# A PEER layer with 112 instead of 96 tokens gathered, and a dense pass over 144 instead of 160

## The reference, cut to what matters

```python
def peer(h, w_pq, sub_keys, u_tab, v_tab):
    qr = (hb @ w_pq).reshape(b, t, PEER_HEADS, 2, PEER_DKEY // 2)
    sc = jnp.einsum('bthpd,hpnd->bthpn', qr, sub_keys)
    s_top, i_top = lax.top_k(sc, PEER_TOPK)                 # 16 of 128, twice
    cand = s_top[..., 0, :, None] + s_top[..., 1, None, :]
    c_top, c_pos = lax.top_k(cand.reshape(b, t, PEER_HEADS, 256), PEER_TOPK)
    ...
    expert = i0 * PEER_NKEYS + i1                           # 8 heads x 16 picks = 128 per token
    g = jax.nn.softmax(c_top, axis=-1)
    a = jax.nn.gelu(jnp.einsum('bthkd,btd->bthk', u_tab[expert], hb))
    return jnp.einsum('bthk,bthkd->btd', (g * a), v_tab[expert])
```

## Time and profile before

| | |
|---|---|
| median of 3 runs | 1709.11 us (1707.29 to 1711.14) |
| profiled execution, its own time | 1709.63 us |
| its span in the trace | 1707.7 us |
| PE busy | 1668.3 us (98%) |
| VectorE busy | 1017.4 us (60%) |
| ScalarE, GpSimd busy | 405.2 us (24%), 262.2 us (15%) |
| moved by DMA | 569.87 MB, 334 GB/s over the span |
| granted TensorE clock | 0.994 |

### The profile page before, as it was taken

How to read it: one execution, slowest core, us unless ns; L and a number is a source line. 1 busy time by engine, 2 the same in 40 slices (tenths; PEclk the granted TensorE clock), 3 DMA queues, 4 the chain that set the end, 5 groups by cost and what they waited for, 6 DMA issues and landing times.

```text
span 1707.7 us, 28225 instructions
## 1 busy us (share of the span) xinstructions
PE 1668.3 (98%) x11296; PEld 1587.6 (93%) x11296; DVE 1017.4 (60%) x1695; ACT 405.2 (24%) x1027; POOL 262.2 (15%) x252
## 2 busy tenths in 40 slices
PE   7999999999999999999999999999989999999999
PEld 6768888888999999999899999999989999999998
DVE  5325695766778999767677676373335443443331
ACT  6547567646441000021112111210000000000000
POOL 1020000000003322231312221031112111111100
PEclk9999999999999999999999999999999999999999
DMA  9665446476548999999999999799999999999995
GB/s 354 215 145 145 127 137 196 137 232 211 173 159 354 422 394 422 405 406 417 393 407 424 397 423 423 296 362 421 422 413 422 422 422 422 422 421 422 422 368 174
DMA packets 106476, 569.87 MB, mean 334 GB/s; under 512 B 11184, under 2 KB 13360, under 8 KB 47472
## 3 DMA queue, kind: packets, MB, share of 16 engines
q1 hardware_dynamic: 56480, 216.51, 34.6%
q0 software_dynamic: 31792, 220.50, 31.9%
q10 hardware_dynamic: 18144, 132.13, 18.9%
HBM read 563.04 MB, written 4.46 MB: 332 GB/s over the span
## 4 chain that ended last, share of the span: by engine, by line
PE 64%; DMA 18%; DVE 13%; issue 2%; POOL 1%; ACT 1%; SPq 0%; DVEq 0%; ACTq 0%; POOLq 0%
PE ps L1516 32%; DMA late<-in_u_rows,sel 8%; PE ps L1461 6%; PE ps L1263 5%; PE ps L1265 5%; PE ps L1264 5%; DMA sel<-sel 5%; DVE late L1097 3%; DMA acts<-in_u_rows,sel 3%; PE ps L1282 2%; PE ps L1419 2%; PE ps L1418 2%; PE ps L1417 2%; DVE w_lo L788 1%; DMA raw<-in_w_in 1%
## 5 line engine op out<-in xcount | busy, mean ns | idle before, releaser
L1101 DVE SCALAR_TENSOR_TENSOR acts<-late,sel,acts 128x2048 f32<-128x2048 f32 x77 | 181.0, 2351 | 240.1 <-DMA late<-in_v_tab,sel 239.6
L1516 PE MATMUL ps<-acts,raw 128*128 (+1 forms) x2048 | 285.8, 301 | 5.9 <-DMA raw<-in_v_tab 5.9
L1461 PE MATMUL ps<-acts,late 128*128 128x160 f32 x2048 | 290.5, 301 | 0.0
L1516 PEld LDWEIGHTS ps<-acts,raw 128*128 128x128 f32 x2048 | 282.2, 191 | 6.1 <-issue 6.1
L1461 PE MATMUL ps<-acts,raw 128*128 128x160 f32 x2048 | 286.7, 299 | 0.0
L1461 PEld LDWEIGHTS ps<-acts,late 128*128 128x128 f32 x2048 | 284.4, 192 | 0.0
L1516 PE MATMUL ps<-acts,late 128*128 (+1 forms) x2048 | 284.2, 299 | 0.0
L1461 PEld LDWEIGHTS ps<-acts,raw 128*128 128x128 f32 x2048 | 280.4, 190 | 0.2 <-DMA raw<-in_u_tab 0.2
L1516 PEld LDWEIGHTS ps<-acts,late 128*128 128x128 f32 x2048 | 280.1, 190 | 0.1
L788 DVE TENSOR_TENSOR w_lo<-raw,w_hi 128x512 fp32r<-128x512 f32 (+1 forms) x288 | 189.0, 683 | 140.8 <-ACT w_hi L530 139.4
L1097 DVE SCALAR_TENSOR_TENSOR late<-late,acts 128x2048 f32<-128x2048 f32 x76 | 173.3, 2289 | 54.3 <-DMA late<-in_u_rows,sel 54.1
(11 more groups left out here) (207 smaller groups left out, 1522.0 us busy)
## 6 DMA issues: line engine op xcount, KB each, us to landing
raw<-in_w_in SPq DMA_DIRECT2D x72, 512.0 KB, 3.7
raw<-in_u_tab SPq DMA_DIRECT2D x33, 1024.0 KB
late<-in_u_tab SPq DMA_DIRECT2D x33, 1024.0 KB
raw<-in_v_tab SPq DMA_DIRECT2D x32, 1024.0 KB
raw<-in_v_tab ACTq DMA_DIRECT2D x32, 1024.0 KB
late<-in_v_tab SPq DMA_DIRECT2D x32, 1024.0 KB
late<-in_v_tab ACTq DMA_DIRECT2D x32, 1024.0 KB
raw<-in_u_tab ACTq DMA_DIRECT2D x31, 1024.0 KB
```

What stands on the lines that cost most here:

```text
L1101: V.scalar_tensor_tensor(acc, row[n % NROW], w_sp[:, n - N_OWN:n - N_OWN + 1], acc, ALU.mult, ALU.add).then_inc(row_used, 1)
L1461: ins = mm(ps[:, q, 0:N_DN], ring[q][:, k * P:k * P + P], hF[:, k, :], start=k == 0, stop=k == KD - 1)
L1516: ins = mm(ps[:, pair_bank(k // 2), at:at + N_DN], ring[q][:, k * P:k * P + P], acts[:, ds(i * (4 * N_DN) + q * N_DN, N_DN)], start=first ...
```

## The change

`SHARE` becomes 8: of eight partitions of tile 0 seven are gathered tokens and one is a helper. That makes 112 gathered and 144 dense tokens, `N_OWN` 112, `N_TURN` 16, seven turns, `N_GRP` 36 and `FIRST_G` 56. So there are 112 gathers of each table and 144 moving columns in each dense matmul. Beside that:

- the gate tables exist twice (`hot1[g % 2]`, `hot0[g % 2]`), and DVE writes those of group g+1 where it wrote those of g;
- 24 rows instead of 6 are taken ahead of the normalisation of the gates;
- a gather of the second table waits, beside its free buffer, until the chunks have come to a given number (from chunk 116 on, 134 chunks for 112 rows);
- the weights of the gathered tokens are made ready at chunk `WEIGH_AT` = 120 instead of 122, and from there one row is taken in each second chunk instead of each one;
- the score tiles lie elsewhere, so that one fill of ones on POOL goes; the turns are written as a loop.

```diff
-    SHARE = 4
+    SHARE = 8
@@
-        hot1 = early[:, 0:512].rearrange("p (t n) -> p t n", t=4)
-        hot0 = early[:, 512:1024].rearrange("p (t n) -> p t n", t=4)
+        hot1 = [at.rearrange("p (t n) -> p t n", t=4) for at in (early[:, 0:512], region(A_TK, 512))]
+        hot0 = [at.rearrange("p (t n) -> p t n", t=4) for at in (early[:, 512:1024], region(A_TK + 512, 512))]
@@
+        WEIGH_AT = NKEY - 8
+        PACE_FROM, PACE_TO = NKEY - 12, 2 * NKEY - 6
@@ def gather(n):
                 if n >= NROW:
                     pool.wait_ge(row_used, n + 1 - NROW)
+                if n >= N_OWN:
+                    pool.wait_ge(unit_used, PACE_FROM + (n - N_OWN) * (PACE_TO - PACE_FROM) // N_OWN)
@@ POOL
-            pool.memset(region(A_SCORE + 2048, 2048), 1.0).then_inc(ones_set, 1)
...
+            def next_turn(first, turn):
+
+                gathers(first, (turn - 1) * N_TURN + NROW - 1)
+                pool.wait_ge(row_used, (turn - 1) * N_TURN)
+                pool.dma_start(hs[turn % 2][helpers, :], hs[turn % 2][lenders[turn], :]).then_inc(hs_in, 16)
...
-            for i in range(2):
+            for i in range(SHARE - 2):
                 pool.wait_ge(turn_kept, i + 1)
                 pool.dma_start(lent[lenders[i], :], acc_copy[helpers, :]).then_inc(lent_in, 16)
@@ DVE
-            next_row(6)
+            next_row(24)
@@ def hots(g):
-                if g:
-                    dve.wait_ge(gate_mm, g)
-                for f, dst in ((1, hot1), (0, hot0)):
+                if g >= 2:
+                    dve.wait_ge(gate_mm, g - 1)
+                for f, dst in ((1, hot1[g % 2]), (0, hot0[g % 2])):
@@
             for c in range(FIRST_G + 4, NKEY):
                 if c % 2 == 0:
-                    hots(g)
+                    if g + 1 < N_GRP:
+                        hots(g + 1)
...
-                if c == NKEY - 6:
+                if c == WEIGH_AT:
...
-                if c > NKEY - 6:
+                if c > WEIGH_AT and c % 2:
                     next_row()
...
-            for turn in range(3):
+            for turn in range(SHARE - 1):
                 next_row(N_OWN + (turn + 1) * N_TURN - rows_done[0])
-                if turn < 2:
+                if turn < SHARE - 2:
```

More of the change, by code:

```diff
@@ L183, in build_block @@
         own_row, help_count = sel[:, 2 * N_PICK + N_OWN:2 * N_PICK + N_OWN + 1], sel[:, 2 * N_PICK + N_OWN + 1:2 * N_PICK + N_OWN + 2]
-        A_SCORE = NKEY * N_DN - TT * 2048
+        A_SCORE = [NKEY * N_DN - 2048, A_ROW + D + 1504]
+        assert A_SUBK + 16 * NKEY <= A_SCORE[0] and A_SCORE[1] + 2048 <= NKEY * SEQ
         A_TK = A_ROW + D
@@ L188, in build_block @@
         A_ONES = FIRST_G * N_DN
-        score = [region(A_SCORE + 2048 * b, 2048).rearrange("p (c n) -> p c n", c=16) for b in range(TT)]
+        score = [region(A_SCORE[b], 2048).rearrange("p (c n) -> p c n", c=16) for b in range(TT)]
         A_SLOT = A_TK
@@ L403, in _ @@
             sp.wait_ge(x2_stored, 16)
-            sp.wait_ge(unit_used, NKEY + 26)
+            sp.wait_ge(unit_used, NKEY + X_CHUNKS)
             sp.dma_start(x_rest[0], io["x2_scratch"][P:SEQ, :]).then_inc(x2_back, 16)
@@ L490, in _ @@
             pool.wait_ge(score_done, 2 * NH)
-            pool.memset(region(A_ONES, A_SCORE - A_ONES), 1.0).then_inc(ones_set, 1)
+            pool.memset(region(A_ONES, A_SCORE[0] - A_ONES), 1.0).then_inc(ones_set, 1)
             gathers(NROW, NROW + 8)
             pool.wait_ge(slot_ready, NH)
-            pool.memset(region(A_SCORE, 2048), 1.0).then_inc(ones_set, 1)
-            gathers(NROW + 8, NROW + 24)
-            pool.wait_ge(slot_ready, 2 * NH)
-            pool.memset(region(A_SCORE + 2048, 2048), 1.0).then_inc(ones_set, 1)
[L498 to L504, removed]
-            for i in range(2):
+            pool.memset(region(A_SCORE[0], 2048), 1.0).then_inc(ones_set, 1)
+            def next_turn(first, turn):
+                gathers(first, (turn - 1) * N_TURN + NROW - 1)
+                pool.wait_ge(row_used, (turn - 1) * N_TURN)
+                pool.dma_start(hs[turn % 2][helpers, :], hs[turn % 2][lenders[turn], :]).then_inc(hs_in, 16)
+            next_turn(NROW + 8, 2)
+            for turn in range(3, SHARE - 1):
+                next_turn((turn - 2) * N_TURN + NROW - 1, turn)
+                if turn == 4:
+                    pool.wait_ge(gsp_ready, 1)
+                    for i, rows in enumerate(lenders):
+                        pool.dma_start(w_sp[helpers, N_TURN * i:N_TURN * i + N_TURN], w_sp[rows, N_OWN:N_PICK]).then_inc(gsp_in, 16)
+            gathers((SHARE - 3) * N_TURN + NROW - 1, N_OWN + N_TURN + NROW - 1)
+            for i in range(SHARE - 2):
                 pool.wait_ge(turn_kept, i + 1)
@@ L509, in _ @@
             pool.wait_ge(row_used, 2 * N_OWN)
-            pool.dma_start(lent[lenders[2], :], acc[helpers, :]).then_inc(lent_in, 16)
+            pool.dma_start(lent[lenders[SHARE - 2], :], acc[helpers, :]).then_inc(lent_in, 16)
         @block.scalar
@@ L754, in _ @@
                     hot_scale(scale_after[c])
-                if c == NKEY - 8:
+                if c == WEIGH_AT - 2:
                     act.wait_ge(row_used, N_OWN)
@@ L1095, in next_row @@
                         if n % N_TURN == 0:
-                            dve.wait_ge(hs_in, 32 if turn < 2 else 48)
+                            dve.wait_ge(hs_in, 16 * max(2, turn + 1))
                         V.scalar_tensor_tensor(row[n % NROW], row[n % NROW], 1.0, hs[turn % 2], ALU.mult, ALU.mult,
@@ L1152, in gate @@
                 if g == 0:
-                    dve.wait_ge(ones_set, 3)
+                    dve.wait_ge(ones_set, 2)
                     dve.wait_ge(gelu_done, FIRST_G)
@@ L1187, in _ @@
             hots(0)
+            hots(1)
             apply(FIRST_G + 1)
@@ L1190, in _ @@
             gate(0)
-            hots(1)
+            hots(2)
             apply(FIRST_G + 2)
@@ L1230, in _ @@
                     dve.wait_ge(acc_set, turn + 2)
-            dve.wait_ge(lent_in, 48)
+            dve.wait_ge(lent_in, 16 * (SHARE - 1))
             V.tensor_tensor(acc, acc, lent, ALU.add).then_inc(acc_sum, 1)
@@ L1476, in gate_group @@
                 for k in range(4):
-                    ins = mm(ps[:, 4 + par, k * P:k * P + P], hot1[:, k, :], hot0[:, k, :], start=True, stop=True)
+                    ins = mm(ps[:, 4 + par, k * P:k * P + P], hot1[par][:, k, :], hot0[par][:, k, :], start=True, stop=True)
                 ins.then_inc(gate_mm, 1)
```

19 lines of the change are left out of this document (10 added, 9 removed).

## The result

| | before | after |
|---|---|---|
| median | 1708.68 us (4 runs) | 1782.41 us (1779.99 to 1784.33, 4 runs) |
| ratio to before | | 1.0429, 95% interval 1.0416 to 1.0443 |
| profiled execution, span | 1709.63 us, 1707.7 us | 1779.99 us, 1778.2 us |
| PE busy | 98% | 88% |
| moved | 569.87 MB | 603.56 MB |

The change makes the kernel 4.3% slower. The forecast was slower, 1768 us with a range of 1742 to 1798.

What follows compares the result with a forecast made beforehand. The prediction took DMA at 422 GB/s as the bound, with TensorE as full: 1697 + 79.5 - 11.7 - 23.0 + 5.0 = 1746.8 us, plus the end, gives 1768 us; range 1742 to 1798.

Steps and rivals of the forecast that it cites:

- The wall: Retrieval stage: the DMA engines can move 422 GB/s, which is 2.485 us per table unit or gathered row.
- The term of 79.5 us for 32 more units: Gathers of both tables: 112 instead of 96 each, 32 x 2.485 us of added DMA time; called the term that decides.
- Narrower matmuls: Dense chunks on TensorE: 4.35 to 3.96 us each, 104 us off with fewer gate groups, useful only if data keep up.
- The seam: Between the two tables' gathered rows: the idle DMA hole of 18.7 us shrinks to 7 us, gaining 11.7 us.
- The end: Stage ends with the last gathered row, not the last chunk; 2 + 9.3 + 5.5 + 2.9 us follow it.
- The rival of slow gathers: Rows left after TensorE's last chunk: gathers alone can't fill the DMA engines; 22 us more, 1790 us; 17% chance.
- The 2 us for a turn's copy that can't be caught up: End of the second table's rows: VectorE's last copy of a turn's sum adds 2 us to the span.
- The clock: TensorE in the v stretch: long waits hold it at its lower clock, 7.9 us a chunk, some 2190 us; 3% chance.
- Together 5.0 us more: Idle DMA time added by lending row numbers: six lendings instead of five, 2.7 us each, one ahead of the gates 5 us.
- the pause: TensorE stopped for tens of us while 24 rows are taken ahead of its gates; costed at nothing by itself.
- my 1746.8: Forecast time in us of the last gathered row: 1697 + 79.5 - 11.7 - 23.0 + 5.0.
- The gate tables: Tables written one group ahead in the u stretch: take away TensorE waits such as 2.99 us; costed at nothing.

Runs made afterwards that it cites:

- e_bytes: Changed kernel, but every seventh gather (32 of 224) brings 64 bytes per partition instead of a row of 8 KB; 1712.68 us, ratio 1.0012.
- e_pe: Changed kernel with two more matmuls of 128 columns in each of the 256 chunks, giving back TensorE's saving; 1781.04 us, ratio 1.041.
- e_nopause: Changed kernel with 6 rows instead of 24 ahead of the gates' normalisation, the 18 others spread over gate chunks; 1771.73 us, ratio 1.0352.
- e_lend: Changed kernel with the helpers' row numbers lent in two pieces instead of seven; 1769.49 us, ratio 1.0346.
- b_ahead: Kernel before the change with only the change's gate tables, two of each, written one group ahead; 1706.74 us, ratio 0.9976.
- b_lend: Kernel before the change with the helpers' row numbers lent in two pieces instead of six; 1706.36 us, ratio 0.9976.
- b_two: Kernel before the change with gate tables one group ahead and numbers lent in two pieces, weights still at chunk 122; 1703.06 us, ratio 0.995.

## Why the prediction was right

*The wall.* 422 GB/s held: no stretch of 50 us or more that was looked at was above it in any run. The term of 79.5 us for 32 more units decided, and `e_bytes` shows it: 69.7 us go with those bytes. The chain of the changed kernel bears this out in part only: from 1172 to 1460 us it goes over TensorE's v chunks (L1528) and waits for dense units, and over gathers from there, where the prediction had it over gathered rows and not over v chunks.

*Narrower matmuls.* 3.96 us a chunk was forecast and 3.92 measured, 104 us less for TensorE and 97. That they are worth nothing is shown by `e_pe`.

*The seam.* 18.7 us of idle time became 0.2 in 1110 to 1180 us; I had left 7.

*The end.* 27 rows alone were forecast and 28 came; TensorE ended at 1694 us where I had 1680, since the dense units came late now and then (11.7 us of waits for them, 9.7 in one). The rival of slow gathers did not come: 2.48 us a row without the operations between the turns, against 2.485. From the start of the last row's use to the end of the span 18.1 us were measured, and 17.7 and 2 forecast. The 2 us for a turn's copy that can't be caught up did not come: behind the last one lay 16 rows, and VectorE waited for a row again at 1742 and 1745 us. (The prediction's 2.43 us a row divides four rows by four; from start to start it is 9.71 less 2.35, by three, 2.45 us.)

*The clock.* The granted clock was 0.99 in 1172 to 1690 us, and this rival did not come either.

*The term that was mis-sized: "Together 5.0 us more"*, the idle time that the lendings add. For 600 to 1110 us the step gave 13.6 + 5.0 = 18.6 us; measured were 3.6 + 16.1 + 10.0 = 29.7. 750 to 830 us alone made 16.1 us of it, where I had put 5 for one lending. That lending cost 6.7 us; 6.5 us more come at the end of the pause, where GpSimd waits for the normalised gates to lend the weights, a wait that I had not counted; 2.9 us lie ahead. The rest of the lendings were costed well, 13.6 us against 3.6 and 10.0. `e_nopause` gives 10.7 us back, and there GpSimd lends the weights without a wait; `e_lend` gives 12.9, but leaves 12.3 us idle in 750 to 830. I had costed the pause at nothing by itself. Its length costs nothing, but it takes away the dense loads under which GpSimd's waits could hide, and it made one such wait.

*The rest of the 14 us.* 1199.9 + 48 us bring the last row to 1760, 13 us behind my 1746.8: 15.7 us more idle time (11.1 of the above, 4.8 in the v stretch at 418 GB/s and 5.6 in the rows alone, where I had none, one more up to 600, and 6.8 less at the seam), less 2.3 us of bytes. The end was 1.6 us shorter. The profiled execution lies 2.4 us under its median, where I had put 0.5 us over it.

*The gate tables.* Costed at nothing inside the change. The prediction said that they take away waits. That is hardly seen: in the changed kernel TensorE waited 30.5 us for gate tables, in the kernel before 12.9, and with the tables alone (`b_ahead`) 13.1. With the numbers lent in two pieces alone (`b_lend`) it was 8.8 us, with both (`b_two`) 5.5. On the kernel before they give 4 us (`b_ahead`), and where these come from stays open.

The Trainium skill, "DMA: Bandwidth & Descriptors", section "Where 436 GB/s comes from", says that for loads from HBM a side of about 358 GB/s per core binds, though it also quotes 425 GB/s measured with 16 MB. The traces here agree with the second figure, not the first: one core alone moved 418 to 422 GB/s for hundreds of us. By the section "Queues, rings and completion order" of that page of the Trainium skill, each engine goes round its queues, so dense loads need not starve beside the gathers. The trace agrees for the most part: TensorE lost 11.7 us in the v stretch to late units.

## What to carry to other kernels

When two engines are full at once, count for each change which of the two it loads: here 97 us were taken off TensorE and 79.5 us put on the DMA engines, and only the second counted. Make the balance in bytes, for the whole stage, with the idle moments as a list of their own; then a change of order is worth the idle time that it closes and not the wait that it removes. And look what ends the next stretch before closing a hole: in the kernel before, 18.7 us of DMA time at the seam were worth nothing, since TensorE ended the v stretch. When an engine is made to pause, list what else waits for the end of the pause: here GpSimd did, and with it the gathers. A small copy that is waited for in a queue full of large gathers should be issued some gathers ahead, all such copies together.

## What was not expected of the hardware

GpSimd's indirect DMA instruction takes 0.94 us, and with room in the ring the next one follows 1.25 us behind (752.76 and 754.01 in the rows above). When gathers are issued one behind the other for long with nothing else loading, it takes 2.15 to 2.2 us, a pace of 2.46 to 2.49 us, which is about that of the transfers (2.485 us). So GpSimd itself is not the bound at 2.46 us; that the transfers hold it back is what this suggests, and was not tried. A ring of five rows alone came to 422 GB/s in 790 to 800 us, and to 388 over the last 70 us, in which a turn ends and the last rows run out. A copy of 1 KB in the gathers' queue took 31 us with dense loads beside it and 7 us with none. And TensorE's granted clock stood at 0.50 in the pause of 60 us, and the chunk behind it cost under a us more.
